# Gated delta rule on one Trainium2 core: query sums with stationary ones, keys' root behind a convolution, and the scan's first decay rows fetched within the in-projection

## The reference, cut to what matters

```python
def _gdn_inputs(qkv, beta_logit, decay_logit, conv_w, a_log, dt_bias):
    qkv = jax.nn.silu(_centred_conv(qkv, conv_w))
    q, k, v = jnp.split(qkv, [GDN_HEADS * GDN_DK, 2 * GDN_HEADS * GDN_DK], axis=-1)
    q = _l2norm(q.reshape(B, T, GDN_HEADS, GDN_DK))   # x * rsqrt(sum(x * x) + eps)
    k = _l2norm(k.reshape(B, T, GDN_HEADS, GDN_DK))
...
def _chunk_gated_delta(q, k, v, g, beta, state0):
    gc = jnp.cumsum(g)                       # within a chunk
    decay = exp(gc[i] - gc[j])               # lower triangle, else 0
    a_mat = strict_lower((k * beta) @ k.T * decay)
    t_mat = inverse(eye + a_mat)
    u, w = t_mat @ (v * beta), t_mat @ (k * beta * exp(gc))
    qk = lower(q @ k.T * decay)
    # per chunk: v_new = u - w @ s;  o = (q * exp(gc)) @ s + qk @ v_new;  s = s * exp(gc_last) + k_dec.T @ v_new
```

## Time and profile before

| | us |
|---|---|
| median of 3 runs (2813.14 to 2823.07) | 2813.27 |
| the profiled execution's own time | 2814.47 |
| its span in the trace | 2812.6 |
| PE busy | 2601.9 (93%) |
| DVE busy | 1643.9 (58%) |
| POOL busy | 1150.0 (41%) |
| ACT busy | 633.1 (23%) |

### The profile page before, as it was taken

One profiled execution on the slowest core, in us unless ns is written; L12 is line 12 of the kernel. 1 busy time (PEld: TensorE's weight loads), 2 busy tenths in 40 slices (PEclk: granted clock), 3 DMA queues, 4 the chain that ended last, 5 costly groups with the idle time before them and its releaser, 6 DMA issues. The chain is left out here.

```text
span 2812.6 us, 45432 instructions
## 1 busy us (share of the span) xinstructions
PE 2601.9 (93%) x18626; PEld 2175.0 (77%) x18626; DVE 1643.9 (58%) x2507; ACT 633.1 (23%) x1229; POOL 1150.0 (41%) x930
## 2 busy tenths in 40 slices
PE   8989999989889999989799979978798999899998
PEld 6778888778568888867788869864686888688887
DVE  7958658472658838667454656533576516563451
ACT  4121111110322101134343344301354100110000
POOL 3544554554044554524331433111333545444453
PEclk9999999999999999989799989989999999999999
DMA  4224343322033334221011101101110222222222
GB/s 155 96 99 154 115 142 136 104 76 75 1 112 135 126 128 148 85 75 46 25 40 47 60 24 41 47 17 38 49 26 31 77 103 90 90 84 96 94 101 75
DMA packets 51317, 229.68 MB, mean 82 GB/s; under 512 B 5297, under 2 KB 12481, under 8 KB 32577
## 3 DMA queue, kind: packets, MB, share of 16 engines
q1 hardware_dynamic: 51136, 227.10, 23.4%
HBM read 224.91 MB, written 2.17 MB: 81 GB/s over the span
## 5 line engine op out<-in xcount | busy, mean ns | idle before, releaser
L246 POOL TENSOR_TENSOR ring_rounded<-ring,ring_rounded 128x512 fp32r<-128x512 f32 (+2 forms) x715 | 935.5, 1340 | 1141.5 <-DVE ring_rounded L237 1133.0
L286 PE MATMUL psum<-arena_rounded,ring_rounded 128*128 128x512 f32 (+1 forms) x2820 | 1100.6, 390 | 61.0 <-PEq L515 13.7
L287 PE MATMUL psum<-arena_rounded,ring_rounded 128*128 128x512 f32 (+1 forms) x2820 | 1091.3, 387 | 0.0
L288 PE MATMUL psum<-arena_rounded,ring_rounded 128*128 128x512 f32 (+1 forms) x2820 | 1090.2, 387 | 0.0
L286 PEld LDWEIGHTS psum<-arena_rounded,ring_rounded 128*128 128x128 f32 x2820 | 536.5, 190 | 182.3 <-issue 45.6
L288 PEld LDWEIGHTS psum<-arena_rounded,ring_rounded 128*128 128x128 f32 x2820 | 536.2, 190 | 107.6
L287 PEld LDWEIGHTS psum<-arena_rounded,ring_rounded 128*128 128x128 f32 x2820 | 536.7, 190 | 104.8 <-issue 1.5
L237 DVE CAST ring_rounded<-ring 128x2048 fp32r<-128x2048 f32 (+4 forms) x191 | 212.3, 1111 | 676.8 <-PE psum L288 618.0
L713 ACT ACTIVATE arena<-psum,vectors 128x512 f32<-128x512 f32 x88 | 68.6, 782 | 409.8 <-PE psum L288 409.8
L329 DVE TENSOR_TENSOR arena_rounded<-arena,arena_rounded 128x512 fp32r<-128x512 f32 (+2 forms) x113 | 125.3, 1109 | 3.9
L327 DVE CAST arena_rounded<-arena 128x512 fp32r<-128x512 f32 (+2 forms) x113 | 114.1, 1010 | 9.3 <-DVE arena L743 1.0
(11 more groups left out here) (403 smaller groups left out, 3058.6 us busy)
## 6 DMA issues: line engine op xcount, KB each, us to landing
ring<-in_w_up SPq DMA_DIRECT2D x44, 1024.0 KB, 4.8
arena<-in_w_mod SPq DMA_DIRECT2D x48, 512.0 KB, 3.4
ring<-in_w_down SPq DMA_DIRECT2D x32, 704.0 KB, 4.0
ring<-in_w_mup SPq DMA_DIRECT2D x16, 1024.0 KB, 4.9
ring<-in_w_mdown SPq DMA_DIRECT2D x16, 1024.0 KB, 4.8
ring<-in_w_gdn SPq DMA_DIRECT2D x12, 1024.0 KB, 4.8
ring<-in_w_lru_in SPq DMA_DIRECT2D x10, 1024.0 KB, 4.8
ring<-in_w_odd_in SPq DMA_DIRECT2D x10, 1024.0 KB, 4.7
```

Source lines behind the costliest of these rows:

```text
L246: last = pool.tensor_tensor(self.rounded(low), raw, self.rounded(high).bitcast(F32), ALU.subtract)
L286: pe.matmul(out, r(wh), r(xh), start=start, stop=False)
L287: pe.matmul(out, r(wh), r(xl), start=False, stop=False)
L288: return pe.matmul(out, r(wl), r(xh), start=False, stop=stop)
```

## The change

1. **Queries' sums.** The ones become stationary (a column spread to 32), the squares move: one matmul of 128x512 a head, head h writing PSUM partitions 32h to 32h + 31. DVE copies the 128x512 result to SBUF, PE transposes its four blocks at (0, 2), and DVE picks the 16 columns and adds eps.
2. **Keys' root** goes behind the taps of unit 4 on DVE (in both groups); POOL's next weight split waits for it as before.
3. **Values' turns** all go beside the first head of unit 5 (k = 2 to 7), ACT copies them out in one run ahead of `tap(us[5], 0)`.
4. **First decays.** After the last turn SP fetches the rows of each direction's first tile within the in-projection, one after the other, into the space of the values before their turn (`VT_AT`), POOL adds the bar there at its end, and ACT ends the stage with an Exp of one column. The scan no longer fetches or bars tile 0, and places its buffers anew.
5. **Kept weights**: DVE's conversion moves from (0, 2) to (2, 2), POOL's from t = 2 to t = 3.

```diff
@@ gdn_in_stage
+        def beside_first(t, k):
+            if k in (1, 3, 5):
+                turn_keys(3 * t + k // 2)
+        def beside_last(t, k):
+            if t == 0 and k >= 2:
+                turn_values(k - 2)
...
-                    if k in (1, 3, 5):
-                        beside(3 * t + k // 2)
+                    beside(t, k)
... act
         tap(us[4], 0)
         tap(us[4], 1)
-        token(6)
-        token(7)
-        token(8)
+        for n in range(NA):
+            token(NA + n)
         tap(us[5], 0)
         silu(us[4], 0)
-        token(9)
         silu(us[4], 1)
-        token(10)
-        token(11)
         tap(us[5], 1)
         silu(us[5], 0)
         silu(us[5], 1)
+        act.activation(m.small[:, 287:288], khalf[:, 0:1], ACT.Exp).then_inc(m.achain.up(), 1)
... dve
-            if unit.u == 4:
-                if bd:
-                    turned()
-                key_roots()
+            if bd and unit.u == 4:
+                turned()
             taps_of(unit, 0)
             taps_of(unit, 1)
...
+        key_roots()
         taps_of(us[5], 0)
... pool
+        for d in range(2):
+            pool.wait_ge(m.sem("rowsin"), m.count("rowsin", 16 * (d + 1)))
+            e = tok.decays[d]
+            pool.tensor_tensor(e, e, m.bar[:, d, :].rearrange(...).broadcast_to([P, GH, P]), ALU.add)
... sp
+        sp.wait_ge(m.sem("turned"), m.count("turned", 2 * NA))
+        for d in range(2):
+            sp.dma_start(tok.decays[d]..., decay_rows(gc_rows, group, SCAN_TILES[d][0], d)).then_inc(...)
+            sp.wait_ge(m.sem("rowsin"), m.count("rowsin", 16 * (d + 1)))
@@ gdn_scan_stage
-        b["EA"] = [m.at(at[4], GH, P), m.at(at[5], GH, P)]
+        b["EA"] = [tok.decays[d], m.at(at[5], GH, P)]
... sp
-        for t in range(2):
-            for d in range(2):
-                decays(t, d)
+        for d in range(2):
+            decays(1, d)
... pe: query_sums
             for h in range(GH):
-                for i in range(NT):
-                    j = NT * h + i
-                    last = pe.matmul(m.psum[:, MB, j:j + 1], qsq[h][:, i * P:(i + 1) * P], m.ones[:, 0:1],
-                                     start=True, stop=True)
+                last = pe.matmul(m.psum[quarter[h], MB, :], m.ones[:, 0:1].broadcast_to([P, 32]), qsq[h],
+                                 start=True, stop=True)
+        def query_turn():
+            pe.wait_ge(m.sem("qrows"), m.count("qrows", 1))
+            for i in range(NT):
+                last = pe.transpose(bank(0, MB)[:, i, :], qsq[0][:, i * P:(i + 1) * P], m.ident[:, :])
+            last.then_inc(m.up("qturned"), 1)
... pe: the loop
                 if (t, k) == (0, 1):
                     query_sums()
+                if (t, k) == (0, 2):
+                    query_turn()
... act: decay
-            act.wait_ge(sem("barred", d), count("barred", d, t + 1))
+            if t:
+                act.wait_ge(sem("barred", d), count("barred", d, t))
... pool
-        barred(0, 0)
-        barred(0, 1)
         first_level(0, 0)
         first_level(0, 1)
...
-            if t == 2:
+            if t == 3:
                 m.pool_kept(pool)
... dve
+        def query_rows():
+            dve.wait_ge(m.sem("qsums"), m.count("qsums", 1))
+            dve.tensor_copy(qsq[0], m.psum[:, MB, :]).then_inc(m.up("qrows"), 1)
+        def query_means():
+            dve.wait_ge(m.sem("qturned"), m.count("qturned", 1))
+            sums = m.psum[:, MB, :].rearrange("p (i h c) -> p i h c", h=GH, c=32)[:, :, :, 0]
+            dve.tensor_scalar(qmean..., sums, EPS, None, ALU.add).then_inc(m.up("qmean"), 1)
...
                 if (t, k) == (0, 1):
-                    dve.wait_ge(m.sem("qsums"), m.count("qsums", 1))
-                    dve.tensor_scalar(qmean, m.psum[:, MB, 0:GH * NT], EPS, None, ALU.add)
+                    query_rows()
                 if (t, k) == (0, 2):
-                    m.dve_kept(dve)
+                    query_means()
                 if (t, k) == (0, 4):
                     query_roots()
+                if (t, k) == (2, 2):
+                    m.dve_kept(dve)
```

More of the change, by code:

```diff
@@ L1516 @@
 KT_AT, QT_AT, VT_AT, S_AT = 12288, 15360, 28672, 31744
+Q_MEAN, Q_ROOT, Q_TMP = 24, 40, 64
 K_SS, K_ROOT, K_TMP, K_LEN, K_HALF = 64, 88, 112, 136, 160
-Q_MEAN, Q_ROOT, Q_TMP = 24, 40, 64
 WORK_AT = 6144
@@ L1523, with decay_rows @@
 GC_ROWS_AT = 17408 + 6 * 96
+SCAN_TILES = [[4, 5, 0, 1, 2, 3], [5, 4, 3, 2, 1, 0]]
+def decay_rows(gc_rows, group, n, d):
+    c = n * 16 + d * 8 + GH * group
+    return bass.AP(tensor=gc_rows.tensor, offset=c * P, ap=[[0, P], [1, GH * P]])
 class TokenTiles:
@@ L1533, in __init__ @@
         self.m = m
+        self.decays = [m.at(VT_AT + GH * P * d, GH, P) for d in range(2)]
         self.k_at = tail[0:4] + own[0:2]
@@ L1809, in pe @@
             else:
-                queries(unit, turn_keys if unit.u == 4 else turn_values)
+                queries(unit, beside_first if unit.u == 4 else beside_last)
             if not bd:
@@ L2031, in pool @@
             m.pool_unit(pool, unit)
+        for d in range(2):
+            pool.wait_ge(m.sem("rowsin"), m.count("rowsin", 16 * (d + 1)))
+            e = tok.decays[d]
+            pool.tensor_tensor(e, e, m.bar[:, d, :].rearrange("p (a b) -> p a b", a=1).broadcast_to([P, GH, P]),
+                               ALU.add).then_inc(m.up("barred"), 1)
     def sp(sp):
@@ L2057, in gdn_scan_stage @@
     tok = TokenTiles(m, group)
-    places = [512 * i for i in range(24)] + [VT_AT + 512 * i for i in range(6)]
-    qsq = [m.at(places[26 + h], T) for h in range(GH)]
+    places = [512 * i for i in range(24)] + [VT_AT + 512 * i for i in range(2, 6)]
+    qsq = [m.at(places[24 + h], T) for h in range(GH)]
     qmean, qroot, qtmp = [m.small[:, a:a + GH * NT] for a in (Q_MEAN, Q_ROOT, Q_TMP)]
@@ L2063, in gdn_scan_stage @@
     for d in range(2):
-        at = places[13 * d:13 * d + 13]
+        at = places[12 * d:12 * d + 12]
         b = {name: m.at(at[i], GH, P) for i, name in enumerate(("ZF", "QE", "R", "KD"))}
-        b["EA"] = [m.at(at[4], GH, P), m.at(at[5], GH, P)]
-        b["QK"] = [m.at(at[6], GH, P), m.at(at[7], GH, P), m.at(at[10], GH, P)]
+        b["EA"] = [tok.decays[d], m.at(at[5], GH, P)]
+        b["QK"] = [m.at(at[6], GH, P), m.at(at[7], GH, P), m.at(at[4], GH, P)]
         b["Z1"], b["ZC"] = m.at(at[8], GH, HB), m.at(at[8] + GH * HB, GH, HB)
         b["XC"], b["YC"] = m.at(at[9], GH, HB), m.at(at[9] + GH * HB, GH, HB)
-        b["S"] = [m.at(at[11], GH, P), m.at(at[12], GH, P)]
+        b["S"] = [m.at(at[10], GH, P), m.at(at[11], GH, P)]
         B.append(b)
-    tiles = [[4, 5, 0, 1, 2, 3], [5, 4, 3, 2, 1, 0]]
+    tiles = SCAN_TILES
+    quarter = [slice(32 * h, 32 * h + 32) for h in range(GH)]
     LEVELS = 5
```

17 lines of the change are left out of this document (8 added, 9 removed).

## The result

The changed kernel takes 2791.53 us (median of 4 runs, 2787.02 to 2791.92) where the kernel before took 2814.28 beside it. The ratio is 0.9909, with a 95% interval of 0.9886 to 0.9931: 25.6 us off the 2813.27 that the forecast started from, 19 to 32 by the interval. The two medians alone differ by less, 22.8 us. The forecast was 17.7 off. Among the runs of the kernel before that stand beside e0 one took 4957.11 us in a slow state, and it is left out of the ratios.

A forecast was written before the change was run, and what follows sets the result against it. Chains across engines, not PE's 93% busy time, were taken to bound these stages. Gains of 10.6 us (group 0) and 7.5 (group 1), less 0.4 for the turns, made 17.7: from 2813.27 to 2795.6 us, range 2790 to 2804.5.

The forecast's parts named there:

- A: End of the in-projection: the stage ends earlier, by 2.3 us in group 0 and 1.9 us in group 1.
- B: Start of the scan: the seed comes at +7.0 us instead of +10.8, a gain of 3.7 us per group.
- C: Queries' sums in the scan: column strips run side by side, gaining 4.6 us in group 0 and 1.9 in group 1.
- The clock rival: Scan's start: TensorE's clock rises one window later in both groups, 6 us slower, 2819.6 us; chance 0.04.
- An earlier clock: A reason given, with the sums' lower bound, for the range's low end of 2790 us; no separate size.
- Strips in a row: Queries' sums: column strips don't run side by side, gain only 8.9 us, 2804.4 us; chance 0.12.
- Another wait at the in-projection's end: Slower fetches or a later split leave the stage's end where it was: gain 13.5 us, 2799.8 us; chance 0.08.
- The table load: Scan's start: the table loads again despite the new Exp, DVE starts 0.6 us later, 2796.8 us; no separate chance.
- the sums' lower bound: Queries' sums: four strips fully side by side take 1.9 us, where the forecast took 2.3 us.

The follow-up runs named there:

- e0: The changed kernel run once more, unaltered: 2790.62 us, ratio 0.9908 to the kernel before.
- e6: The changed kernel with the values' turns three beside each head again and ACT's tokens between the Silus: 2793.15 us.
- e1: The kernel before with only the new queries' sums added: 2805.32 us, ratio 0.9964.
- e2: The changed kernel with the old one-column queries' sums put back: 2804.64 us.
- f2: The changed kernel with the old queries' sums, repeated on another chip: 2807.48 us.
- e4: The changed kernel without the one-column Exp at the in-projection's end, so the scan loads the table: 2790.12 us, ratio 0.9915.
- e9: The changed kernel with the old queries' sums and extra unused matmuls at the in-projection's end and behind the scan's first gram: 2794.17 us.
- f4: The changed kernel with the old queries' sums and the extra unused matmuls, repeated on another chip: 2794.73 us.
- e8: The changed kernel with extra unused matmuls at the in-projection's end and behind the scan's first gram: 2785.87 us.
- e12: The changed kernel with the same extra unused matmuls, a second time on another chip: 2786.74 us.
- f3: The changed kernel with the same extra unused matmuls, a third time on another chip: 2786.51 us.
- e11: The changed kernel run again, unaltered, on a third chip: 2792.73 us.

## Why the prediction came out as it did

**Direction: right. Mechanism: right for A and B, incomplete for C.** Faster was the likeliest case, and each part does what the change says; but the gain of C was worked out without the largest thing that changed there, the clock.

**(A): right.** 2.3 and 1.9 us forecast. Measured: the scan's start moves from 22.89 us behind the anchor to 20.63, 2.26; group 1, 1.9 after its clock dip of 1.6 is taken off. The chain that ends the stage is the one named, ACT with the load, POOL 0.7 us before it, and the Exp lands at 1337.43, which is the forecast's 1336.7 plus the 0.7 that this execution was late already. The turns, too, work as thought; e6 shows that without them the fetches end the stage 0.3 us later, which is below what a time can tell. The 0.2 a group that the sum charged was for the four transposes of the new sums, and it was not needed in group 0: PE still waits 0.47 us for the mask behind them.

**(B): right.** Triangle at +2.0 forecast, +2.15 measured; seed at +7.0, +7.16 in both groups. Gain 3.6 and 3.5, forecast 3.7 each.

**(C): the step that failed.** The sum had "4.6 us" for group 0 and "1.9 us" for group 1, at the clock that the earlier trace rows show, "partly faster clock may add to that". Two things are in it. The price of the strips was nearly right: 2.3 us at 0.50 forecast, 1.93 measured at 0.50 (group 1). But for group 0 the clock was held constant across the change. The old sums run at 0.50 for 6.98 us and leave the clock there until 1369, by windows of one microsecond. With the strips it rises at 1349.7, 1 us into them (1.52 us in place of 1.93), and what follows runs at 1.00 but for one dip. To the second mask that made 6.9 and 3.1 us in place of 4.6 and 1.9, and 2.8 more by the last mask of group 0. Undone or done alone, C as a whole is worth 10.1 us in the kernel before (e1) and 14.0 and 14.2 in the changed one (e2, f2), the turns of its result included, not 6.1. With these terms the forecast's own sum reads 4.2 + 7.4 + 10.1 = 21.7 to 4.2 + 7.4 + 14.0 = 25.6, and 23 to 26 was measured. Since the parts don't add up one by one, this shows the size of the missing term and no more.

**The clock rival had the sign wrong.** It said that the change "takes steady work away there" and that the clock could rise a window later. The row it leaned on, 7 us of steady sums at 0.50, was a hint of the opposite: in it the clock did not rise beside this work. Group 1 had a second hint: there it was 1.00 while the old sums ran and 0.50 behind them, where `right` takes 1.13 us. The forecast used the first only against the rival, as a reason that nothing would be lost, and not for the question of what would happen if work of another form stood there. "An earlier clock" appears, but only as a reason for the range's low end, at 2790, without a price.

**The others.** Strips in a row: excluded by 1.52 us for eight. Another wait at the in-projection's end: excluded; the second fetch landed at 1332.0, and the split ended at 1334.4. The table load: the scan has none, and e4 shows that a second one would have cost 0.42 us at the seed.

**The range.** Its low end, 5.6 us under the forecast, had room for the sums' lower bound (0.8 us by the forecast's rates) and some 5 us of an earlier clock; C alone missed by 4 to 8. Four medians of the changed kernel, 2790.6 to 2793.3, lie inside it, but the kernel before was 0.6 to 3.1 us slower in those groups than in the forecast's base; against that base the first result is 2.3 us outside by the ratio and 0.5 us inside by the medians. So the range was met or missed by less than the runs scatter, while the term C was too small by every measure taken.

## What to carry to other kernels

When a change replaces PE work in a stretch at a granted clock of 0.50, ask which form of record stands there, not only how long it is busy: here the clock stayed at 0.50, or fell to it, beside 32 records of one column though PE was busy throughout, and it was up soon where eight of 512 columns stood instead. Price then everything up to the place where the clock used to rise, at both levels, as a case of its own with its own chance. And where several edits meet at one barrier, undo each on its own: what they give singly (30 us) is not what they give together (23 to 26).

## What the runs showed of the hardware

- The granted clock falls under full load: 1.00 when 32 one-column matmuls begin, 0.50 when they end 4.04 us later, with PE busy for 5.00 us of 5.00 (e9; f4 repeats it in both groups). Whether strips of 512 columns raise the clock, or only don't hold it down, no run tells: it rose before, within and behind them.
- The same sums take 6.98 us at 0.50, 4.04 us when they start at 1.00 and 3.73 us when they run at 1.00 to their end (group 1 of e9), so one-column records follow the clock too.
- Matmuls that compute nothing of use, placed where PE would idle, made the whole kernel 5 to 7 us faster by the medians (e8, e12, f3).
- Four column strips of full height run 3.4 times as fast as the same eight records over the full width (1.06 against 3.60 us).
- The kernel's single run moves by up to 11 us between executions (2786.65 to 2797.76 in e11). The anchor alone lies at 1318.51 us in e9 and at 1315.49 in f4, two executions of one kernel. Where the clock rises in group 1's scan differs from run to run too: the strips take 1.06 us there in e0 and 1.93 in the first trace of the changed kernel.
